# Input units as split one-pass products with low halves made by GpSimd, and an S5 readout from four product planes

## The reference

```python
def trunk_layer(x, pos, s5_re0, s5_im0, ret_s0, conv_prev, sb_attend, p):
    h = x @ p['w_in']
    u_a, q_b, k_b, v_b, q_c, k_c, v_c, g_c = jnp.split(h, list(np.cumsum(SPLITS)[:-1]), axis=-1)
    ya, s5r, s5i = s5_branch(u_a, ...)
    yb = sb_attend(q_b, k_b, v_b, p['sb_bias'])
    yc, ret_s = retention_branch(q_c, k_c, v_c, g_c, pos, ret_s0, p['gn_g'], p['gn_b'])
    mix = jnp.concatenate([rms_norm(ya), rms_norm(yb), yc], axis=-1) @ p['w_out']
    x = layer_norm(ALPHA * x + mix, p['ln1_g'], p['ln1_b'])
    f, conv_new = conv_ffn(x, conv_prev, p['w_up'], p['conv_w'], p['conv_b'], p['w_down'])
    return layer_norm(ALPHA * x + f, p['ln2_g'], p['ln2_b'])
```

## Time and profile before

| | |
|---|---|
| median of 3 runs | 674.38 us (674.27 to 674.45) |
| the profiled execution | 674.94 us, its span 673.1 us |
| TensorE busy | 661.4 us, 98% |
| VectorE busy | 569.1 us, 85% |
| ScalarE busy | 415.2 us, 62% |
| GpSimd busy | 91.2 us, 14% |
| granted TensorE clock | 1.000 |

### The profile page before, as it was taken

The page is one execution under the profiler, slowest core; times in us unless marked ns, Lnnn a source line. Parts: engine busy times, 40 slices in busy tenths (PEclk is TensorE's granted clock), DMA queues, the critical chain, the costliest instruction groups (busy, mean ns, idle before and its releaser), DMA issues. The chain is left out here.

```text
span 673.1 us, 13390 instructions
## 1 busy us (share of the span) xinstructions
PE 661.4 (98%) x5024; PEld 613.4 (91%) x5024; DVE 569.1 (85%) x1195; ACT 415.2 (62%) x690; POOL 91.2 (14%) x90
## 2 busy tenths in 40 slices
PE   8999999999999999999999999999999999999997
PEld 6777887989999999999987787989999999999996
DVE  5999999989998988789588998898999898884653
ACT  5776348758676666655847536786867666663343
POOL 0000010150222222200200000106012222220001
PEclk9999999999999999999999999999999999999999
DMA  8777540746674655664456463354765556555411
GB/s 315 244 274 220 188 130 6 274 112 227 203 255 151 201 187 184 197 192 142 142 179 228 167 206 125 115 200 167 199 211 197 188 170 193 176 196 190 161 57 66
DMA packets 42915, 121.82 MB, mean 181 GB/s; under 512 B 5538, under 2 KB 15170, under 8 KB 42338
## 3 DMA queue, kind: packets, MB, share of 16 engines
q1 hardware_dynamic: 40466, 115.22, 51.7%
q0 software_dynamic: 1088, 4.11, 2.5%
q10 hardware_dynamic: 1296, 1.63, 0.8%
HBM read 115.33 MB, written 5.61 MB: 180 GB/s over the span
## 5 line engine op out<-in xcount | busy, mean ns | idle before, releaser
L1579 DVE TENSOR_TENSOR w_lo<-ring,w_hi 128x1024 fp32r<-128x1024 f32 x144 | 175.4, 1220 | 30.6 <-ACT w_hi L964 29.0
L439 PE MATMUL ps<-x_hi,w_hi 128*128 128x264 f32 x672 | 191.0, 284 | 1.0 <-DVE x_lo L1529 1.0
L440 PE MATMUL ps<-x_lo,w_hi 128*128 128x264 f32 x672 | 190.4, 283 | 0.0
L441 PE MATMUL ps<-x_hi,w_lo 128*128 128x264 f32 x672 | 190.3, 283 | 0.0
L964 ACT CAST w_hi<-ring 128x1024 fp32r<-128x1024 f32 x144 | 150.2, 1043 | 59.4 <-PE ps L441 58.7
L439 PEld LDWEIGHTS ps<-x_hi,w_hi 128*128 128x128 f32 x672 | 126.5, 188 | 1.9 <-issue 1.8
L440 PEld LDWEIGHTS ps<-x_lo,w_hi 128*128 128x128 f32 x672 | 126.6, 188 | 0.0
L441 PEld LDWEIGHTS ps<-x_hi,w_lo 128*128 128x128 f32 x672 | 126.0, 188 | 0.0
L432 PE MATMUL ps<-x,ring 128*128 128x264 f32 x480 | 112.1, 390 | 0.1
L432 PEld LDWEIGHTS ps<-x,ring 128*128 128x128 f32 x480 | 89.1, 190 | 18.9 <-issue 2.2
L439 PE MATMUL ps<-hff_hi,w_hi 128*128 128x264 f32 x352 | 100.0, 284 | 0.0
(11 more groups left out here) (364 smaller groups left out, 1091.0 us busy)
## 6 DMA issues: line engine op xcount, KB each, us to landing
ring<-in_units SPq DMA_DIRECT2D x187, 512.0 KB, 3.5
kv<-in_kpool SPq DMA_DIRECT2D x32, 128.0 KB, 2.4
kv<-in_vpool SPq DMA_DIRECT2D x32, 128.0 KB, 2.4
SR<-in_sret SPq DMA_DIRECT2D x2, 1024.0 KB, 5.9
out_rsample<-SR POOLq DMA_DIRECT2D x2, 1024.0 KB, 5.1
out_kv<-hb ACTq DMA_DIRECT2D x2, 528.0 KB, 4.4
VBC<-v_rows POOLq DMA_DIRECT2D x8, 128.0 KB, 3.5
out_y<-x SPq DMA_DIRECT2D x3, 264.0 KB, 2.1
```

Source lines behind the costliest of these rows:

```text
L439: mm(out, wh, hi, start=start, stop=False)
L440: mm(out, wh, lo, start=False, stop=False)
L441: return mm(out, wl, hi, start=False, stop=stop)
L1579: E.did(tt(w_lo[:, slot], ring[:, ring_slot(L * UNITS + i)], w_hi[:, slot].bitcast(F32), ALU.subtract), "w_lo")
```

## The change

`EARLY` holds units 8 to 19 of layer 0 and 6 to 19 of layer 1. Their high parts go to eight places that are free for a while (`HOMES`: VBC, Oh, prev and VT, later planes of `work`); three or so units share each, and ScalarE makes the high part of unit j behind the copy of unit j - 3. The low halves of the weights (two instructions of 128 x 512 per unit) and of x (two of 128 x 1056) move from VectorE to GpSimd, with a semaphore `pool_mix` for TensorE. `xe_lo` lies over `hb` from unit 12's place on, so ScalarE copies it to `turn` (`late_x`) before unit 12 is copied out, and units from 13 on use the copy. `prev` is loaded behind unit 18 (layer 0) or 16 (layer 1) rather than behind unit 12. `s5_c` reads P2, P1, P4 and P3 themselves, four planes with the factors `cf[0]`, its negative, `cf[1]` and `cf[1]`; the two sums in `s5_post` go, and `sfin` is made of the last columns. `s5_pre(0, 1)` waits for `s5y` before P2 and P4 as well; in layer 1 these two products go to `tabs[0]`. The core of the diff; left out are counts of semaphores and the removed VectorE functions `split_lo_early` and `lower_early`, which stand with GpSimd now:

```diff
-EARLY = [[], [16, 17, 18, 19]]
+EARLY = [list(range(8, 20)), list(range(6, 20))]
+LATE_X = 13
+X_LATE_AT = [11, 9]
+HOMES = [{8: "VBC", 9: "Oh", 10: "prev", 11: "VBC", 12: "Oh", 13: "prev", 14: "VBC", 15: "Oh", 16: "VT", 17: "VBC",
+          18: "Oh", 19: "P2"},
+         {6: "VBC", 7: "Oh", 8: "prev", 9: "VBC", 10: "Oh", 11: "prev", 12: "VBC", 13: "Oh", 14: "VT", 15: "VBC",
+          16: "BR", 17: "BI", 18: "P1", 19: "P2"}]
+HI_AT = [lambda j: 18 if j == 19 else j - 3, lambda j: RAW if j == 19 else j - 3]
+PREV_AT = [18, 16]
...
-        xe_lo = at("xe_lo", [P, KT, T], over=("work", 4 * HJ * T), dt=F32R)
+        VTc = at("VTc", [P, 2, HEADS * DV], over=("work", 4 * HJ * T))
+        rg = work[:, 5]
-        rg = turn[:, 0]
         xe_hi = at("xe_hi", [P, KT, T], over=("z", 0), dt=F32R)
+        xe_lo = [at("xe_lo0", [P, KT, T], over=("hb", VC * T), dt=F32R),
+                 at("xe_lo1", [P, KT, T], over=("turn", 0), dt=F32R)]
...
+        we_hi = {home: at(f"we_{home}", [P, 8, P], over=where, dt=F32R)
+                 for home, where in (("VBC", ("VBC", 0)), ("Oh", ("Oh", 0)), ("prev", ("prev", 0)), ("VT", ("VT", 0)),
+                                     ("BR", ("work", 0)), ("BI", ("work", HJ * T)), ("P1", ("work", 2 * HJ * T)),
+                                     ("P2", ("work", 3 * HJ * T)))}
...
-                sp.dma_start(prev[:], A["prev"][L]).then_inc(S("ld_prev"), 16)
                 for i in range(13, UNITS):
                     unit(L, i)
                     if i < 17:
                         pages(L, "vpool", i - 13, 4)
+                    if i == PREV_AT[L]:
+                        sp.dma_start(prev[:], A["prev"][L]).then_inc(S("ld_prev"), 16)
...
             def tile8_split(L, i, out):
 
-                n, wh = L * UNITS + i, we_hi[EARLY[L].index(i)]
-                wait_low(pe, L, i)
+                n, wh, xl = L * UNITS + i, home_of(L, i), xe_lo[i >= LATE_X]
+                pe.wait_ge(S("pool_mix"), pool_count(L, 5 + 2 * EARLY[L].index(i)))
+                if i == LATE_X:
+                    pe.wait_ge(S("x_hi"), x_count(L, 0))
                 for k in range(8):
-                    if i == EARLY[L][0] and k in (0, KT // 2):
-                        pe.wait_ge(S("x_lo"), L * KT + 1 + k // (KT // 2))
                     wl = ring_lo[:, ring_slot(n), k]
                     mm(out, wh[:, k], xe_hi[:, k], start=(k == 0), stop=False)
-                    mm(out, wh[:, k], xe_lo[:, k], start=False, stop=False)
+                    mm(out, wh[:, k], xl[:, k], start=False, stop=False)
                     ins = mm(out, wl, xe_hi[:, k], start=False, stop=(k == 7))
                 E.did(ins, "used")
...
             def s5_c(L, hf):
-                need(pe, "s5x", L, hf + 1)
+                need(pe, "s5rd", L, hf + 1)
...
-                for c, X in enumerate((P1, P3)):
+                for X, factor in ((P2, cf[:, 0]), (P1, cft[:, 0]), (P4, cf[:, 1]), (P3, cf[:, 1])):
                     for jj in range(HJ):
-                        mm(bank[32 * jj:32 * jj + 32, 0:SEQ], cf[:, c, hf * HJ + jj], X[:, jj, 0:SEQ],
-                           start=(c == 0), stop=(c == 1), tile_position=(0, 32 * jj))
+                        mm(bank[32 * jj:32 * jj + 32, 0:SEQ], factor[:, hf * HJ + jj], X[:, jj, 0:SEQ],
+                           start=(X is P2), stop=(X is P3), tile_position=(0, 32 * jj))
...
-                need(act, "s5rd", L, 2)
-                need(act, "qk", L, 1)
-                E.did(nc.scalar.copy(we_hi[EARLY[L].index(i)][:], ring[:, ring_slot(n)]), "w_hi")
+                home, former = HOMES[L][i], home_before(L, i)
+                if former is not None:
+                    tile_done(act, L, former)
+                elif home == "VBC":
+                    needr(act, "rawh", 2 * L, RAW)
+                elif home == "prev" and L > 0:
+                    act.wait_ge(S("st_prev"), 16 * L)
+                elif home == "VT":
+                    need(act, "tph", L, 2)
+                elif home in ("BR", "BI", "P1", "P2"):
+                    need(act, "s5y", L, 2)
+                    need(act, "qk", L, 1)
+                E.did(nc.scalar.copy(home_of(L, i)[:], ring[:, ring_slot(n)]), "w_hi")
+
+            def late_x(L):
+
+                if L == 0:
+                    need(act, "s5rd", L, 1)
+                else:
+                    need(act, "s5x", L, 1)
+                act.wait_ge(S("pool_mix"), pool_count(L, 3))
+                for t in (0, KT // 2):
+                    E.did(nc.scalar.copy(xe_lo[1][:, t:t + KT // 2], xe_lo[0][:, t:t + KT // 2]), "x_hi")
...
+                    if i == VC:
+                        act.wait_ge(S("x_hi"), x_count(L, 0))
                     E.did(nc.scalar.copy(hb[:, i], ps[:, in_bank(i), 0:T]), "in_evac")
...
+                    for j in EARLY[L]:
+                        if i == HI_AT[L](j) and i > RAW:
+                            split_hi_early(L, j)
+                    if i == X_LATE_AT[L]:
+                        late_x(L)
                     for hf in range(2):
                         for c in range(2):
                             if i == at_[f"b{hf}{c}"]:
                                 s5_evac(L, hf, c)
                     if L == 0 and i == RAW + 1:
                         s5_tables(0, 0)
+                        upper_early(L)
+                    if L > 0 and i == RAW:
+                        upper_early(L)
+                        split_hi_early(L, EARLY[L][0])
...
                         E.did(nc.scalar.mul(SR[:], SR[:], gam[:, 0:1]), "srg")
-                        if EARLY[L]:
-                            upper_early(L)
...
-                        for e in EARLY[L]:
-                            split_hi_early(L, e)
...
                         if L > 0:
                             square_a(L)
+                            split_hi_early(L, EARLY[L][-1])
                             split_hi(L, N_IN)
...
-                E.did(tt(cf[:, 1], cf[:, 1], cft[:, 1], ALU.subtract), "cf")
+                E.did(tt(cf[:, 1], cf[:, 1], cft[:, 1], ALU.subtract))
+                E.settle()
+                E.did(ts(cft[:, 0], cf[:, 0], -1.0, None, ALU.mult), "cf")
...
+                A, B = tabs[0] if L > 0 and hf == 1 else (P2[:, :, tm], P4[:, :, tm])
                 need(dve, "tab", L, 2 * hf + 2)
                 need(dve, "buev", L, 2 * hf + 1)
-                E.did(tt(P2[:, :, tm], TC, BR[:, :, tm], ALU.mult))
-                E.did(tt(P4[:, :, tm], TS, BR[:, :, tm], ALU.mult))
+                if L == 0 and hf == 1:
+                    need(dve, "s5y", L, 1)
+                E.did(tt(A, TC, BR[:, :, tm], ALU.mult))
+                E.did(tt(B, TS, BR[:, :, tm], ALU.mult))
...
-                E.did(tt(P1[:, :, tm], P2[:, :, tm], P1[:, :, tm], ALU.add))
-                E.did(tt(P3[:, :, tm], P3[:, :, tm], P4[:, :, tm], ALU.subtract))
+                E.did(tt(P1[:, :, tm], A, P1[:, :, tm], ALU.add))
+                E.did(tt(P3[:, :, tm], P3[:, :, tm], B, ALU.subtract), "s5x" if hf == 1 else None)
...
                 E.did(tt(P4[:, :, tm], TS, BR[:, :, tm], ALU.mult))
                 E.did(tt(P3[:, :, tm], TC, BI[:, :, tm], ALU.mult), "s5rd")
                 E.settle()
-                E.did(tt(P1[:, :, tm], P2[:, :, tm], P1[:, :, tm], ALU.subtract))
-                E.did(tt(P3[:, :, tm], P3[:, :, tm], P4[:, :, tm], ALU.add))
-                E.settle()
-                E.did(cp(sfin[:, 0, jr], P1[:, :, SEQ - 1]))
-                E.did(cp(sfin[:, 1, jr], P3[:, :, SEQ - 1]), "s5x")
+                E.did(tt(sfin[:, 0, jr], P2[:, :, SEQ - 1], P1[:, :, SEQ - 1], ALU.subtract))
+                E.did(tt(sfin[:, 1, jr], P3[:, :, SEQ - 1], P4[:, :, SEQ - 1], ALU.add))
...
                 rotary(L)
                 sb_mask(L)
-                if EARLY[L]:
-                    lower_early(L, 0)
                 ret_inner(L)
                 keys_decayed(L)
                 s5_out(L)
                 s5_finals(L)
-                if EARLY[L]:
-                    split_lo_early(L, EARLY[L][0])
                 sb_out(L)
-                if EARLY[L]:
-                    lower_early(L, 1)
                 conv_prev(L)
-                for e in EARLY[L][1:]:
-                    split_lo_early(L, e)
...
+                tile_done(pool, L, max(j for j in EARLY[L] if HOMES[L][j] == "VBC"))
...
+            def lower_early(L, half):
+
+                t = half * KT // 2
+                pool.wait_ge(S("x_hi"), L * (KT + 4) + half + 1)
+                E.did(tt(xe_lo[0][:, t:t + KT // 2], x[:, t:t + KT // 2], xe_hi[:, t:t + KT // 2].bitcast(F32),
+                         ALU.subtract), "pool_mix")
+
+            def split_lo_early(L, i):
+
+                pool.wait_ge(S("w_hi"), split_count(L, i))
+                slot, hi = ring_slot(L * UNITS + i), home_of(L, i)
+                for k in (0, KT // 2):
+                    part = slice(k, k + KT // 2)
```

(44 more changed lines are left out.)

2 lines of the change are left out of this document (1 added, 1 removed).

## The result

The changed kernel takes 724.79 us (median of 4 runs, 723.74 to 725.50) beside 674.41 for the kernel before (4 runs, 674.27 to 674.84): 1.0745 times as long, 95% interval 1.0726 to 1.0763. The profiled execution took 724.61 us, its span is 722.8, its mean granted TensorE clock 0.967.

A forecast was written before the change was run, and what follows sets the result against it. VectorE, neck and neck with TensorE, was taken to bound the input stages, with GpSimd's subtractions taking turns on its port. 674.4 + 25.6 (layer 0) + 19.3 (layer 1) = 719.3, said as 719 us; range 697 to 730.

The forecast's parts named there:

- (D): Clock falls to 1.2 GHz in four input-stage idle stretches: 4 to 8 us more, 723 to 727; within forecast's 0.76.
- The port term: Input stages: each 512-column GpSimd subtraction holds VectorE up 1.05 us (bounds 0.93 and 1.25), an x half 2.3.
- Layer 0 (1): Before the first readout's products: two x halves and low halves of units 8 to 12 come in between, 15.1 us.
- (2): Layer 0: second `s5_pre` waits for readout and BI, +4.0; layer 1: units 10 to 15 before `sb_second`, 12.6 less 2.3.
- (3): Layer 0: units 15 to 18 before second readout, +8.4; layer 1: second readout, sums dropped, planes added, -1.6.
- (4): Layer 0 second readout: dropped sums, TensorE's planes and order, -0.9; layer 1: units 13 to 15 0.66 shorter each, -2.0.
- (5): Layer 0: units 18 and 19 are 0.66 us shorter, 19 partly behind the group norm, -1.0.
- Layer 1 (1): Before the first readout: two x halves and low halves of units 6 to 9, 13.0 us.
- The sum: Input stages of both layers: +25.6 us in layer 0 and +19.3 in layer 1.
- (A): Rival, input stages: the port is shared but VectorE's scans pass freely, 16.8 us less, 702; chance 0.12.
- (B): Rival: no price on the port; layer 0 +2.3, layer 1 wins 3.2, together 673.5, the same; chance 0.06.
- (C): Rival, input stages: TensorE leads and VectorE's waits are slack, 664, faster; chance 0.06.

The follow-up runs named there:

- the run with layer 1 late: Changed kernel with only units 16 to 19 of layer 1 split, their low halves and x's by GpSimd: 709.12 us, ratio 1.0501.
- the filled kernel: Changed kernel plus matmuls that only keep TensorE at work ahead of its four long waits: 721.09 us, ratio 1.0691.
- The memset kernel: Changed kernel with GpSimd's 56 low-half subtractions replaced by memsets to zero, which read nothing: 676.51 us, ratio 1.0034.
- the free units: Changed kernel with the old S5 readout and GpSimd's low halves as memsets: 678.93 us, ratio 1.0065.

## Why the prediction held, point by point

The forecast was 719, the range 697 to 730, the result 724.8: the forecast's mechanism, at the value that (D) gave for it (723 to 727).

- **The port term** of 1.05 for 512 columns is what the scans show (1.63 apart less 0.58). An x half cost 2.08 and 2.23 in layer 0 (starts 3.22 and 3.48 apart, 1.14 and 1.25 before), and the two together 4.35 in the run with layer 1 late, against 2.3 each. The worry named last, GpSimd's instructions falling into the settling gaps, did not come true: VectorE was slowed once per GpSimd instruction in each row of them.
- **Layer 0 (1)**, 15.1 us: the products ended at 76.15, for 76.5 forecast; against 61.45 before, with the start 0.31 earlier, that is 15.0, with 0.33 for the factor's negation in it, which the forecast priced beside the sum. **(2)**, 4.0: 3.9. The first pair started 5.8 behind the products in place of 4.4, since the readout ran at the lower clock, but the BI pair, held by ScalarE, started 10.9 behind them as forecast, which hid that. **(3)**, 8.4: 8.2.
- **(4)**, -0.9, came out as +0.7: the clock. The tails started at 109.39 at half speed, and `yd` waited 2.95 us for the readout behind them. In the filled kernel, where the clock is at 1.00 there, the same interval is 9.44 us (109.84 to 119.28), 0.8 shorter than before. **(5)**, -1.0, was wrong at either clock: 0.0. Between `yd` and the norms VectorE was the bound in layer 0, not TensorE, and a half of unit 19 met its mask (126.38: 1.76 us for 0.68). The memset kernel, where the mask takes its 0.68, has -0.05 there, so the shorter units bring nothing without that meeting either.
- **Layer 1 (1)**, 13.0: 12.6. **(2)**, 12.6 less 2.3: together +10.95, but by other parts. The wait for the first readout, which "costs nothing more", cost 2.65 us at the lower clock and ate the 2.3; and 10 halves met VectorE, not 12, as two fell into that wait. At the full clock these parts came out at -1.6 and +12.0, for -2.3 and +12.6. **(3)**, -1.6: -1.1 with the tails at half speed, -2.2 at the full clock. **(4)**, -2.0, was wrong at either clock: -0.25. The forecast booked the two planes' 1.07 at `yd`, where VectorE hid them: before, the readout ended at 402.16 and `yd` started at 403.84; after, `yd` starts when the readout ends. So what TensorE saves in units 13 to 15 pays first for these 1.7 us of lead that it has lost.
- **The sum**, 44.9, fell 4.8 short of the 49.7 between the two spans (50.4 between the medians). Two terms were mis-sized for want of asking who leads behind `yd`: (5) of layer 0 by 1.0 and (4) of layer 1 by 1.75. Most of the rest is the clock.
- **(D)** was right in its rows: the granted clock fell to 0.50 in all four waits (from 410 to 415 us too). Its price, 4 to 8, is 3.7 by the filled kernel, which left one readout of layer 0 at a clock of 0.83; the forecast's whole total with it is right in part because the two mis-sized terms make up what it lacks. The Trainium skill (TensorE: Matmul & The Clock Gate, What's actually happening) says that an idle array falls back to the slower level; the trace agrees, 0.50 in the window from 65 to 70 us.
- **(A)** fell: scans wait like products. **(B)** is the memset kernel: 676.5 against 673.5. By the traces layer 1 gave -3.0 for -3.2 there, but by other parts: -0.9 at the BI pair, -2.4 at `yd` and nothing behind it, where (B) had -2.0 for the shorter units. Layer 0 added 5.0 for 2.3: VectorE's `yd` waits 3.18 us for the readout, with a clock of 0.72 in the tails' window there too (86 to 92 us). **(C)** fell twice, in the free units and in the memsets.
- GpSimd's pace was not the bound (TensorE waited 3.3 us for `ring_lo` in both layers together), and the moved loads cost nothing that the table shows. TensorE's idle time, 26 and 23 us, was less than the 30 a layer that the forecast named.

No version here beats the kernel before. The nearest, the new readout in layer 1 alone, is slower by 0.1% or more.

## What to carry to other kernels

GpSimd is no free engine beside a VectorE that works on two SBUF operands: price its instruction by what it holds the other up, here 1.05 us for a half that VectorE makes in 0.57, and give it only what it can do in VectorE's waits, or what reads nothing. Where two engines run neck and neck, taking work off one buys no more than the wait that the other shows (0.52 us here), and moving work between them needs both sides priced. When an edit turns waits into idle stretches of TensorE, add what the matmuls behind them cost at the lower clock, but ask of each stretch whether another wait hides it.

## What the runs showed of the hardware

- What a GpSimd instruction costs the VectorE instruction that it meets: 2.1 to 2.2 us for a subtraction of 1056 columns, 1.05 for 512, 0.49 for 256, so some 2 ns a column with hardly anything fixed; 0.37 for a copy of 512; nothing for a memset of 512, which itself takes 0.5.
- The hold is shorter than the instruction: two subtractions of 512 columns with nothing beside them take 2.50 to 2.53 us, 1.25 each, and cost 1.05 each.
- Scans with a broadcast operand pay as much as products.
- A TensorE that had idled for 9 us ran at half its speed when work came back (records of 0.42 at 0.22 apart from 70.20 on, 0.12 apart from 74.92 on), at a granted clock of 0.50 while it waited.
